# A reverse scan split at the diagonal block, and row loads queued one tile earlier, in a hybrid decoder step

## The reference

```
z[t,s]   = q[t].k[s]/sqrt(64) + bias[h]                  visible where s < t
keep     = sigmoid(-z)                                   1 where not visible
A[t,s]   = sigmoid(z[t,s]) * prod_{s<j<t} keep[t,j]      0 where not visible
o_sb[t]  = sum_s A[t,s] v[s]
mix      = concat(rmsnorm(o_gdn)*norm_g*silu(z_gdn), o_sb*silu(z_sb)) @ w_out
y        = layernorm(2**0.25 * h + mix) * g + b
```

## Time and profile before

| what | value |
|---|---|
| three runs, median (range) | 2954.98 us (2950.54 to 2958.71) |
| the profiled execution: its time, its span | 2954.24 us, 2952.4 us |
| busy in the span: PE, DVE, ACT, POOL | 85%, 44%, 29%, 26% |
| prompt attention, first scan to last product | 1741.5 to 2371.0 us |
| merge, to the end of the span | 2609 to 2952.4 us |

### The profile page before, as it was taken

The page is one execution under the profiler, slowest core; times in us unless marked ns, Lnnn a source line. Parts: engine busy times, 40 slices in busy tenths (PEclk is TensorE's granted clock), DMA queues, the critical chain, the costliest instruction groups (busy, mean ns, idle before and its releaser), DMA issues. The chain is left out here.

```text
span 2952.4 us, 37477 instructions
## 1 busy us (share of the span) xinstructions
PE 2501.9 (85%) x14073; PEld 1579.6 (54%) x14073; DVE 1308.9 (44%) x1766; ACT 848.4 (29%) x1605; POOL 779.1 (26%) x479
## 2 busy tenths in 40 slices
PE   5999899996899995999999658878878768868887
PEld 3555444443344444888888635655555545633333
DVE  1111165666000003555555138797887934412222
ACT  2222032222000001223222027575757612210000
POOL 2433011001000003445343024444444400013433
PEclk9999899998899997999999559998989989989899
DMA  5232211210222211111010171130400059953222
GB/s 153 89 103 82 47 30 44 67 52 21 53 81 74 50 61 55 29 43 43 28 43 22 41 163 33 30 72 8 94 8 23 5 203 339 346 172 97 88 98 71
DMA packets 161789, 233.30 MB, mean 79 GB/s; under 512 B 16496, under 2 KB 95361, under 8 KB 156568
## 3 DMA queue, kind: packets, MB, share of 16 engines
q1 hardware_dynamic: 161688, 231.93, 26.1%
HBM read 162.97 MB, written 68.91 MB: 79 GB/s over the span
## 5 line engine op out<-in xcount | busy, mean ns | idle before, releaser
L1536 DVE TENSOR_TENSOR_SCAN f_keep<-f_keep,f_first 128x144 f32<-128x144 f32 (+15 forms) x128 | 441.2, 3452 | 18.8 <-ACT f_a L1508 18.8
L613 PE MATMUL ps<-hT,wa 128*128 128x512 f32 (+1 forms) x960 | 354.4, 532 | 39.1 <-DMA wa<-w_in 38.4
L1590 POOL TENSOR_TENSOR f_a<-f_a,f_keep 128x144 f32<-128x144 f32 (+15 forms) x128 | 288.1, 2255 | 349.1 <-DVE f_keep L1536 349.1
L447 PE MATMUL ps<-hT,wc 128*128 128x512 f32 (+1 forms) x960 | 355.2, 532 | 12.5 <-DMA wc<-w_in 12.5
L613 PEld LDWEIGHTS ps<-hT,wa 128*128 128x128 f32 x960 | 168.6, 191 | 224.9 <-issue 224.9
L447 PEld LDWEIGHTS ps<-hT,wc 128*128 128x128 f32 x960 | 168.9, 191 | 198.0 <-issue 198.0
L2001 PE MATMUL ps<-m_w,m_mT 128*128 128x512 f32 x544 | 255.3, 631 | 0.0
L1456 PE MATMUL ps<-con,f_a 128*128 128x128 f32 x1216 | 195.2, 300 | 55.9 <-DVE f_at L1544 30.5
L321 PE MATMUL ps<-wt,hT_now 128*128 128x512 f32 x544 | 237.3, 594 | 0.0
L1456 PEld LDWEIGHTS ps<-con,f_a 128*128 128x128 f32 x1216 | 141.8, 150 | 143.8 <-POOL f_a L1590 47.0
L1440 PE MATMUL ps<-f_k,f_q 64*128 64x344 f32 (+19 forms) x832 | 184.5, 529 | 35.7 <-DMA f_k<-chan 34.6
(11 more groups left out here) (276 smaller groups left out, 3261.5 us busy)
## 6 DMA issues: line engine op xcount, KB each, us to landing
j_kp<-cache_k SPq DMA_DIRECT2D x128, 256.0 KB, 4.0
j_v<-cache_v SPq DMA_DIRECT2D x128, 256.0 KB, 4.7
chan<-y SPq DMA_DIRECT2D x12, 1088.0 KB, 6.0
chan<-ya SPq DMA_DIRECT2D x12, 1088.0 KB, 10.6
d_ld<-chan SPq DMA_DIRECT2D x16, 768.0 KB, 5.4
h_rows<-hg SPq DMA_DIRECT2D x17, 512.0 KB, 5.0
m_hh<-h_rows SPq DMA_DIRECT2D x17, 512.0 KB, 3.3
f_k<-chan SPq DMA_DIRECT2D x16, 516.0 KB, 14.7
```

The costliest lines, as they stand in the source:

```text
L447: m = pe.matmul(ps[:, ci, 0:n], wc[k][:, c, :], hT[:, c, c0:c0 + n], start=(c == 0), stop=(c == KC - 1))
L613: m = pe.matmul(ps[:, ci, 0:n], wc[k][:, c, :], hT[:, c, c0:c0 + n], start=(c == 0), stop=(c == KC - 1))
L1536: dve.tensor_tensor_scan(x, x, first[:, L - n:L][:, ::-1], 0.0, ALU.mult, ALU.add).then_inc(scanned, 1)
L1590: pool.tensor_tensor(w, w, keep[i % KEEPS][:, L - n + 1:L + 1], ALU.mult).then_inc(weighed, 1)
```

## The change

The scan of a step becomes two instructions. The first covers the 128 columns of the diagonal block and has the identity, reversed, as second operand. The second covers the remaining n - 128 columns with multiply and bypass; it names the tile itself as second operand and starts from the last value of the first, for which DVE waits on a new semaphore. The array `first` and the two instructions that filled it (L1559, L1560) go. In the merge the rows of tile t+1 are loaded at the place where those of tile t were.

```diff
+    diagonal = p.sem("diagonal_scanned")
...
-        first = sb("first", P, L)
...
-                dve.tensor_tensor_scan(x, x, first[:, L - n:L][:, ::-1], 0.0, ALU.mult, ALU.add).then_inc(scanned, 1)
+                dve.tensor_tensor_scan(x[:, 0:P], x[:, 0:P], p.ident[:, ::-1], 0.0, ALU.mult, ALU.add).then_inc(diagonal, 1)
+                dve.wait_ge(diagonal, START + i + 1)
+                dve.tensor_tensor_scan(x[:, P:n], x[:, P:n], x[:, P:n], keep[i % KEEPS][:, L - P:L - P + 1], ALU.mult, ALU.bypass).then_inc(scanned, 1)
...
-            dve.memset(first[:, 0:SEQ + N_META - P], 0.0)
-            dve.tensor_copy(first[:, L - P:L], p.ident)
...
             load_h(1)
+            load(2)
             for t in range(2, NT):
-                load(t)
+                if t + 1 < NT:
+                    load(t + 1)
                 load_mixed(t)
                 load_h(t)
                 store(t - 2)
```

## The result

The changed kernel takes 2903.45 us (median of four runs, 2899.98 to 2907.34) against 2954.56 us: a ratio of 0.9827, 95% interval 0.9806 to 0.9849, or 51 us less. Forecast were 2914 us, 40 us less; the time lies in the range. Its profiled execution has a span of 2905.0 us, 47.4 less than before.

The account below looks back on a forecast made before the run. Scan and POOL product alternating were taken to bound the attention, a store-load-mix-layer norm loop the merge. Scan +27 and merge -67 us gave -40 us, from 2954.2 to 2914 us; range 2896 to 2938, chance 0.82.

Parts of the forecast that it names:

- (f): Merge: DVE's and POOL's own round, layer norm to mix, takes 13.2 us a tile once the loads come earlier.
- (g): Merge: PE's turn and products take 14.5 us a tile and become the bound, at full clock; -67 us.
- (a) to (c): Attention: diagonal scan 0.407 us, 0.04 us wait, then the rest; the pair costs 0.255 us more than the old scan.
- (c): Attention: the rest scan over n - 128 columns keeps 2.087 ns a column, with some 0.06 us more for its start value.
- What lies on the path: Attention: 88 scans of 784 columns or wider pay the whole 0.255 us, 22 us; 40 narrower pay half, 5 us.
- (d): Attention: the scan's stall behind POOL's products moves into the diagonal and stays as long; gain 0 to 11 us, taken as 0.
- (e): Attention's head: removing the fill of `first` (1.67 us and a like copy) gains nothing, hidden by the first keys' load.
- Rival 1: Attention: all 129 us of the scans' stall behind POOL's products go too; 2785 us, chance 0.03.
- Rivals 2 and 4: Merge: 2, loads still land on the round, 2949 us, chance 0.06; 4, merge does not move, 2981 us, chance 0.03.
- rival 3: Attention: the second scan takes half again as long a column, 1.04 ns more, 130 us; 3044 us, chance 0.06.

Follow-up runs that it names:

- the run with fewer products: The changed kernel with two of the eight chunks of each merge product left out, 24 matmuls a tile instead of 32; 2880.20 us, 0.9756.
- the run of the scan alone: The kernel before with only the scan split in two and its merge loads left as they were; 2978.22 us, 1.0089.
- the run of the merge alone: The kernel before with only the merge's row loads moved one tile earlier and the single scan kept; 2883.64 us, 0.9763.

## Why the prediction was right

**The merge, (f) and (g).** Right in mechanism: the loop of store, load and mix left the chain, PE became the bound with the full clock, and DVE's and POOL's round came next at 13.0 us (13.2 forecast), as the run with fewer products shows. The size was a little off: turns came 14.17 us apart, not 14.5. I had taken the turn's 0.50 and the products' 13.90 us with a gap; in the chain after they are 0.44 and 13.73 with none, and 14 x 0.33 = 4.6 us, less 1.0 us by which the merge came later to tile 2's turn, explains the -71 for -67.

**The price of the pair, (a) to (c).** Right: POOL's idle time before the widest product grew by 0.25 us (4.39 to 4.64), 0.255 forecast. Of the two readings of the earlier trace rows the one taken holds: the same 2.08 ns a column, and 0.218 instead of 0.139 us fixed. The upper price in (c), 0.255 us + 0.125 ns x 464, comes to 0.313 us and not 0.32, which takes 1 us off the upper end.

**What lies on the path.** Here the sum was mis-sized. Between the ends of successive products, added up by width, the 88 steps of 784 columns and more took 20.7 us longer in the changed kernel (22 forecast), the narrower ones 1.3 us less (5 more forecast), and 1.8 us more in the run of the scan alone. In the run of the merge alone, whose scan is the old one, the same sums moved by -2.4 and +0.2 us. On balance the narrow steps pay nothing for the longer pair, not half, within this scatter: +19.3 in place of +27. Why is not shown; 12 of them, in which the diagonal came in ahead of a product, grew by 6.0 us, and the others fell by 7.3.

**The stall, (d).** Right: it moved into the diagonal. These take 187.7 us where 128 x 0.409 = 52 would be free, so 135 us of standing, and the rests another 17 (304.4 against 287.6 when free). That the rest leaves POOL free did not hold either, and it would have been worth 12.6 us of the attention, as the rest's PSUM operand showed. The count of steps in which the diagonal comes in ahead of the product was too small: in the trace 19 rests stand more than 0.1 us over their free length, the widest in a step of 1808 columns, where (d) had 11 steps of at most 912. The gain taken for them, 0, holds all the same, because in these steps the rest stood instead: with the step behind each they took 8.5 us longer in sum. The rests' mean of 2.38 us was forecast as 2.25, without those 17 us. By the rule of the Trainium skill, page "SBUF — State Buffer", section "SBUF: two separate sides", a scan with one SBUF input would not stand behind a product. The runs with PSUM operands agree: such diagonals took 0.42 us at most, such rests 4.25.

**The cover, (e).** Right: without the fill DVE only stood idle longer before the first scan, 13.84 us instead of 10.71, until ACT had the first gates; PE waited 34.7 us for the first keys, where it had waited 34.6.

**The rivals.** Rival 1 (the stall goes) falls with the diagonals of over 3 us; what it asked for takes both operands out of SBUF. Rivals 2 and 4 fall with the turns at 14.17 us, rival 3 with 2.083 ns a column. The whole, -51 against -40, is 11 us too small: 4 us from the merge, 6 us from the narrow steps and 1 us from the wide ones. Both errors lie on the same side, so the range was not met by luck of two that cancel.

## What to carry to other kernels

When an instruction's length scatters for one shape, put its rows beside those of the other engines: a scan of 144 columns at 0.44 and 3.73 us gave away the turn-taking with POOL that no semaphore names. Here splitting it helped only where the part that goes first was free of POOL. All with the new loads of the merge, the kernel took 0.9763 of the time of before with the scan left whole, 0.9807 with only the long rest's operand in PSUM, 0.9707 with only the diagonal's, and 0.9498 with both. Ask which part meets the other engine, not how large the freed part is. And a load that waits for a store only because both stand in one queue can cost as much as a whole loop: here moving it by one tile gave 70 us and showed PE as the bound.

## What was not expected of the hardware

A scan takes turns with POOL even for an operand that it names and does not use: with multiply and bypass and the tile named twice, a rest of 16 columns took 3.02 us beside a product and 0.25 us alone. A column of PSUM in the same place, repeated over up to 1936 columns, costs nothing (at most 4248 ns at 1936 columns, where the tile itself took 4251 on average) and lets both engines run. These rests still take their start value from a column of the SBUF tile, and that alone did not make one stand.
